# One attention unit per half tile instead of one per tile, in a hybrid mLSTM and windowed-attention layer

## The reference

```
u = rmsnorm(x) * (1 + scale) + shift
aq, ak, av, az, mq, mk, mv, mo, mz, mg, ga, gb = split(u @ w_in)      # 2048 -> 11792 columns
att = windowed attention of 16 query heads / 4 key heads x 64, sink logit, latents also see all context keys
y_b = att * silu(az)
y_a = bidirectional mLSTM(mq, mk, mv, gates mg), 4 heads x 256, head norm, * sigmoid(mo) * silu(mz)
merged = sigmoid(ga) * (y_a @ w_proj_a) + sigmoid(gb) * (y_b @ w_proj_b)
y = x + gate * rmsnorm(merged @ w_out)
```

## Time and profile before

| | us |
|---|---|
| median of 3 runs | 2192.31 |
| the profiled execution's own time | 2192.95 |
| its span | 2191.2 |
| TensorE busy in the span | 2115.9 |
| VectorE, ScalarE busy | 869.0, 643.8 |

### The profile page before, as it was taken

One profiled execution on the slowest core, in us unless ns is written; L12 is line 12 of the kernel. 1 busy time (PEld: TensorE's weight loads), 2 busy tenths in 40 slices (PEclk: granted clock), 3 DMA queues, 4 the chain that ended last, 5 costly groups with the idle time before them and its releaser, 6 DMA issues.

```text
span 2191.2 us, 33985 instructions
## 1 busy us (share of the span) xinstructions
PE 2115.9 (97%) x13450; PEld 1965.6 (90%) x13450; DVE 869.0 (40%) x1674; ACT 643.8 (29%) x1046; POOL 109.4 (5%) x188
## 2 busy tenths in 40 slices
PE   5889999999999999999999979999999999999997
PEld 1559999989999999999999979999999999997885
DVE  5875655432224223322322234343434533352223
ACT  5763122232223332332332221313131422231221
POOL 2001000000000000000000000000000100000001
PEclk9999999999999999999999999999999999999998
DMA  8873765542233224222422243535252644423223
GB/s 299 271 241 112 214 176 169 168 117 82 84 109 92 76 76 127 85 78 76 128 76 76 77 124 78 158 84 158 80 152 85 197 125 124 118 86 125 77 77 144
DMA packets 295171, 274.07 MB, mean 125 GB/s; under 512 B 17921, under 2 KB 243961, under 8 KB 292641
## 3 DMA queue, kind: packets, MB, share of 16 engines
q1 hardware_dynamic: 282416, 218.21, 35.2%
q0 software_dynamic: 12656, 54.40, 6.7%
HBM read 232.65 MB, written 39.92 MB: 124 GB/s over the span
## 4 chain that ended last, share of the span: by engine, by line
PE 92%; DVE 3%; DMA 2%; ACT 1%; issue 1%; SPq 1%; DVEq 0%; POOL 0%; ACTq 0%; POOLq 0%
PE bank L1432 45%; PE bank L1438 22%; PE bank L1651 10%; PE bank L1526 2%; PE bank L1347 2%; PE bank L1402 2%; PE bank L1575 2%; PE bank L1566 1%; PE bank L1577 1%; PE bank L1386 1%; PE bank L1499 1%; DVE WL L893 1%; DMA Y<-in_x_prompt_dram 1%; PE bank L1481 1%; DVE XL L893 1%
## 5 line engine op out<-in xcount | busy, mean ns | idle before, releaser
L1432 PE MATMUL bank<-XH,WH 128*128 128x320 f32 x3392 | 788.1, 314 | 5.5 <-ACT WH L639 4.5
L1432 PE MATMUL bank<-XL,WH 128*128 128x320 f32 x3392 | 773.8, 309 | 0.0
L875 DVE TENSOR_TENSOR WL<-RAW,WH 128x1024 fp32r<-128x1024 f32 x244 | 298.8, 1225 | 988.9 <-ACT WH L639 988.3
L639 ACT ACTIVATE WH<-RAW 128x1024 fp32r<-128x1024 f32 x244 | 258.3, 1059 | 1170.9 <-PE bank L1438 1013.6
L1432 PEld LDWEIGHTS bank<-XH,WH 128*128 128x128 f32 x3392 | 565.6, 188 | 14.1 <-ACT WH L639 5.4
L1432 PEld LDWEIGHTS bank<-XL,WH 128*128 128x128 f32 x3392 | 568.2, 188 | 0.0
L1438 PE MATMUL bank<-XH,WL 128*128 128x320 f32 x3392 | 532.2, 309 | 0.0
L1438 PEld LDWEIGHTS bank<-XH,WL 128*128 128x128 f32 x3392 | 506.2, 188 | 0.0
L1651 PE MATMUL bank<-WH,XH 128*128 128x512 f32 x320 | 127.8, 399 | 3.4 <-DVE WL L875 2.5
L1651 PE MATMUL bank<-WH,XL 128*128 128x512 f32 x320 | 124.7, 390 | 0.0
L1651 PE MATMUL bank<-WL,XH 128*128 128x512 f32 x320 | 124.6, 389 | 0.0
(11 more groups left out here) (196 smaller groups left out, 1510.2 us busy)
## 6 DMA issues: line engine op xcount, KB each, us to landing
RAW<-in_w_in_dram SPq DMA_DIRECT2D x180, 512.0 KB, 4.9
proj_dram<-OUTS POOLq DMA_DIRECT2D x92, 320.0 KB, 3.9
WORK<-in_w_ada_dram SPq DMA_DIRECT2D x54, 512.0 KB, 4.2
RAW<-in_w_ada_dram SPq DMA_DIRECT2D x42, 512.0 KB, 5.2
RAW<-in_w_out_dram SPq DMA_DIRECT2D x32, 512.0 KB, 3.9
WORK<-proj_dram SPq DMA_DIRECT2D x20, 640.0 KB, 4.8
WORK<-proj_dram POOLq DMA_DIRECT2D x32, 320.0 KB, 4.9
RAW<-in_w_proj_a_dram SPq DMA_DIRECT2D x16, 512.0 KB, 4.1
```

The source lines that it names most:

```text
L639: nc.scalar.activation(WH[:, gs % 2, :], RAW[:, slot, :], ACT.Copy).then_inc(hi_done, 1)
L875: V.tensor_tensor(WL[:, gs % 2, :], RAW[:, gs % 4, :], WH[:, gs % 2, :].bitcast(F32), ALU.subtract).then_inc(lo_done, 1)
L1432: pe.matmul(banks[n][:, 0:HALF_TOK], wh[:, k, :], x[:, k0 + k, n * HALF_TOK:(n + 1) * HALF_TOK], start=(first and k == 0 and wi == 0), sto ...
```

## The change

L1 shrinks from 12 to 8 tiles per pass. The 16 tiles that it gives up are run in a plain loop of four times four tiles (`T_LM`) between L0 and L1, with no attention beside them. All 10 units of a head stay in its pass, now one per half: in half s TensorE runs S of unit s-3, the first half of the high products, T of unit s-4, the second half of the high products, A of s-4, the low products, O of s-4. O goes into `ab[3]` and no longer `ab[0]`. VectorE runs `gated` of s-5 first, then `row_max` of s-3, then `lo`, then `normalise` of s-4 and `denominators` of s-3; ScalarE runs `soft` of s-3 and `copy_pt` of s-4 in every half. `RDEN` has two places. SyncE's wait for the gate sums now stands behind the loads of the plain loop.

```
-T_L0, T_L1, T_L2, T_MERGE, T_OUT, T_END = 2, 18, 66, 90, 106, 122
-L1_TILES, L2_TILES = 12, 6
+T_L0, T_LM, T_L1, T_L2, T_MERGE, T_OUT, T_END = 2, 18, 34, 66, 90, 106, 122
+L1_TILES, L2_TILES = 8, 6
...
@@ SyncE
             with sp.Fori(1, 4) as ch:
                 l0_body(ch)
+            with sp.Fori(0, 4) as j:
+                for k in range(4):
+                    in_tile(T_LM + k, 4 * j, 512 * j + (COL_M + P * k))
             sp.wait_ge(gada_used, 32)
...
@@ ScalarE
-                    if s >= 3 and s % 2 == 1 and (s - 3) // 2 < 10:
-                        soft((s - 3) // 2)
-                    if s >= 4 and s % 2 == 0:
-                        copy_pt((s - 4) // 2)
+                    if 0 <= s - 3 < 10:
+                        soft(s - 3)
+                    if 0 <= s - 4 < 10:
+                        copy_pt(s - 4)
...
@@ VectorE
                 for s in range(2 * L1_TILES):
-                    lo(kv, 2 * L1_TILES, 2 * T_L1 + s + 1)
+                    if 0 <= s - 5 < 10:
+                        gated(s - 5)
                     if s == 2:
                         prepare()
                         z_gate()
...
+                    if 0 <= s - 3 < 10:
+                        row_max(s - 3)
+                    lo(kv, 2 * L1_TILES, 2 * T_L1 + s + 1)
+                    if 0 <= s - 4 < 10:
+                        normalise(s - 4)
+                    if 0 <= s - 3 < 10:
+                        denominators(s - 3)
...
@@ TensorE, scores: one wait fewer; probs_transposed: one more; out_transposed: another bank
-                    if u >= 2:
-                        pe.wait_ge(yb_done, 10 * kv + u)
...
+                        pe.wait_ge(yb_done, 10 * kv + u + 1)
...
-                    if u < 9:
-                        pe.wait_ge(neg_max, 10 * kv + (u + 2))
-                    transpose(ab[0][:, 0:P], OB).then_inc(ot_psum, 1)
+                    transpose(ab[3][:, 0:P], OB).then_inc(ot_psum, 1)
...
+                    if 0 <= s - 3 < 10:
+                        scores(s - 3)
+                    if x == 0:
+                        pe.wait_ge(out_ready, L1_TILES * kv + (T_L1 + t - 1))
+                    pe.wait_ge(hi_done, done)
+                    high_products(banks, x, 8 * x, range(0, 4), x == 0)
+                    if 0 <= s - 4 < 10:
+                        probs_transposed(s - 4)
+                    high_products(banks, x, 8 * x, range(4, 8), x == 0)
+                    if 0 <= s - 4 < 10:
+                        attend(s - 4)
+                    pe.wait_ge(lo_done, done)
+                    low_products(banks, x, 8 * x, x == 1).then_inc(w_used, 1)
+                    if 0 <= s - 4 < 10:
+                        out_transposed(s - 4)
```

More of the change, by code:

```diff
@@ L243, in hybrid_layer @@
         RT = work(512)
-        MX = work(8)
-        NM, SE, RSUM, RDEN = MX[:, 0:2], MX[:, 2:4], MX[:, 4:6], MX[:, 6:8]
+        MX = work(10)
+        NM, SE, RSUM, RDEN = MX[:, 0:2], MX[:, 2:4], MX[:, 4:6], [MX[:, 6:8], MX[:, 8:10]]
         MXR = work(2)
@@ L561, in _ @@
                     spill(T_L0 + k, 4 * ch, 4 * ch + (4 + k))
+            with pool.Fori(0, 4) as j:
+                for k in range(4):
+                    spill(T_LM + k, 4 * j, 4 * j + (RB_MQ + k))
             pool.wait_ge(gacc_stored, 16)
@@ L570, in _ @@
                 for k in range(L1_TILES):
-                    row = RB_GA + k + 2 * g if k < 2 else RB_MQ + (k - 2) + 10 * g
+                    row = RB_GA + k + 2 * g if k < 2 else RB_MQ + (16 + k - 2) + 6 * g
                     spill(T_L1 + k, L1_TILES * g, row)
@@ L731, in _ @@
                     hi(ch, 8, 2 * (T_L0 + k) + 1)
-            hi(0, 0, 2 * T_L1)
+            hi(0, 0, 2 * T_LM)
+            with act.Fori(0, 4) as j:
+                for k in range(4):
+                    evac(4 * j, T_LM + k - 1)
+                    hi(j, 8, 2 * (T_LM + k) + 1)
+                    hi(j, 8, 2 * (T_LM + k) + 2)
             with act.Fori(0, KV_HEADS) as kv:
@@ L1025, in _ @@
                 gates.leave(4)
-            lo(0, 0, 2 * T_L1)
+            lo(0, 0, 2 * T_LM)
+            with dve.Fori(0, 4) as j:
+                for k in range(4):
+                    lo(j, 8, 2 * (T_LM + k) + 1)
+                    lo(j, 8, 2 * (T_LM + k) + 2)
             with dve.Fori(0, KV_HEADS) as kv:
@@ L1075, in denominators @@
                     dve.wait_ge(probs, 10 * kv + (u + 1))
-                    chain.link(V.tensor_tensor(RDEN, RSUM, SE, ALU.add))
-                    chain.link(V.reciprocal(RDEN, RDEN))
+                    chain.link(V.tensor_tensor(RDEN[u % 2], RSUM, SE, ALU.add))
+                    chain.link(V.reciprocal(RDEN[u % 2], RDEN[u % 2]))
                 def normalise(u):
@@ L1098, in _ @@
                         z_gate()
-                    if s % 2 == 0 and s >= 6:
-                        gated((s - 6) // 2)
-                    if s % 2 == 1 and s >= 5:
-                        normalise((s - 5) // 2)
-                    if s % 2 == 1 and 3 <= s < 23:
-                        row_max((s - 3) // 2)
-                        denominators((s - 3) // 2)
-                gated(9)
+                    if 0 <= s - 3 < 10:
[5 more added lines that the diff above has]
+                        denominators(s - 3)
                 chain.leave(KV_HEADS)
@@ L1420, in _, with high_products @@
                     start_tiles(g, j, part)
-            def product(banks, wslot, k0, done, first, last, k_wait=None):
+            def high_products(banks, wslot, k0, ks, first):
                 wh = WH[:, wslot, :].rearrange("p (k n) -> p k n", k=8)
-                wl = WL[:, wslot, :].rearrange("p (k n) -> p k n", k=8)
-                pe.wait_ge(hi_done, done)
-                for k in range(8):
-                    if k_wait is not None:
-                        pe.wait_ge(k_wait, k0 + k + 1)
+                for k in ks:
                     for wi, x in enumerate((XH, XL)):
@@ L1434, in product, with low_products @@
                                       start=(first and k == 0 and wi == 0), stop=False)
-                pe.wait_ge(lo_done, done)
+            def low_products(banks, wslot, k0, last):
+                wl = WL[:, wslot, :].rearrange("p (k n) -> p k n", k=8)
                 for k in range(8):
@@ L1441, in product @@
                 return ins
+            def product(banks, wslot, k0, done, first, last, k_wait=None):
+                pe.wait_ge(hi_done, done)
+                for k in range(8):
+                    if k_wait is not None:
+                        pe.wait_ge(k_wait, k0 + k + 1)
+                    high_products(banks, wslot, k0, (k,), first)
+                pe.wait_ge(lo_done, done)
+                return low_products(banks, wslot, k0, last)
             def half(i2, i, t, x, k_wait=None):
@@ L1470, in _ @@
                 l0_chunk(ch)
+            with pe.Fori(0, 4) as j:
+                for k in range(4):
+                    for x in range(2):
+                        half(8 * j, 4 * j, T_LM + k, x)
             pe.wait_ge(cols_done, 1)
```

22 lines of the change are left out of this document (8 added, 14 removed).

## The result

The changed kernel took 2198.86 us (median of 7 runs, 2195.24 to 2200.11); the kernel before took 2190.96 us beside it (7 runs, 2189.12 to 2193.3). The ratio is 1.0032 with an interval of 1.0021 to 1.0044. **The change makes the kernel slower by 0.32%.** The forecast was 2187.8 us with a range of 2181 to 2198, so both the sign and the range were missed. The profiled execution took 2199.19 us, 6.2 us more than the one of before (2192.95).

What follows compares the result with a forecast made beforehand. TensorE, busy 97% of the span, was taken as the bound, so only its idle or slow time could be gained. Terms: -3.8 - 0.7 + 0 + 0 + 0 = -4.5 us, giving 2187.8 us, range 2181 to 2198.

Steps and rivals of the forecast that it cites:

- Term 1: End of L0: next weights no longer queue behind the store that waits for all gate sums; gain 3.8 us.
- Term 2: First attention loads before the first `prepare`: idle 2.65 instead of 3.38 us, gain 0.7 us; later groups gain nothing.
- Term 5: Return of TensorE's attention loop: the instruction-fetch stall stays; taken as 0, bounds 0 to 3.4 us gained.
- Term 3: Attention steps on TensorE: passages between kinds of step cost the same; taken as 0, bounds -6 to +6 us.
- Term 4: Chain of a unit, now in one half: `copy_pt` ends 0.9 us before A is due; no cost.
- The rival that I had chosen for the slower side: In each unit half, A waits for the copied probabilities; 2208 us at an excess of 0.5 us; chance 0.15.
- the repeat of the loop fits: At the attention loop's returns, 2086 instructions stay on the chip and stalls go: 2184.4 us; chance 0.13.
- the gain of term 1 is not kept: First attention loads meet traffic or longer half clock, or units pay another 0.1 us passage: about 2192 us; chance 0.22.

Runs made afterwards that it cites:

- The first experiment: Changed kernel with SyncE holding a pass's attention loads until the weights of its second half are converted, about 1.4 us into the pass: 2188.45 us.
- the body of 1878: Changed kernel with the low products left out in 8 of the 16 L1 halves of a pass, 512 products fewer: 2141.73 us.
- the body of 1622: Changed kernel with the low products left out in all 16 L1 halves of a pass, 1024 products fewer: 2089.96 us.
- the eighth experiment: Changed kernel with TensorE's attention loop written out and late attention loads, plus S of the next unit moved behind A: 2183.33 us.
- the kernel with added traffic: Kernel before, with SyncE copying 4 times 655 KB DRAM to DRAM after the last weights of each attention pass: 2223.53 us.
- the body of 2006 instructions: Changed kernel without the low products of halves 0, 1, 14 and 15 of every attention pass, 256 products fewer: 2167.79 us.

## Why the prediction was wrong

- **Term 1 was right.** The low products of L0 and the plain loop are 7.04 us apart from 405 to 665 us; the 3.8 us are gone. The store on ScalarE's queue shows that they are had without moving a tile.
- **Term 2 was right for the first group** in direction: 2.1 us for the 0.7 forecast, since the slow stretch became shorter too, which lay in its bounds. **The step that failed is its last sentence**: that the loads of the later groups can now begin at s = 14, and "nothing is gained". The start was foreseen to the half; what I asked was only what the loads gain. I didn't ask what else uses the DMA engines at that moment, though two groups of rows on my own list said that instructions are fetched through them there.
- **Term 5 failed with it.** I took 0 "since ... the stall did not depend on the work beside it". Before, there was no work beside it: the loads were issued from 643.92, as the stall ended, and the packet moved alone, so the trace of before could not show a dependence either way. Nothing in it excluded a loss, yet my bounds were 0 to 3.4 us gained. The term measured +10.4 us: 5.9 of idle time and 4.5 of slow clock. The first experiment takes it back with one wait; the written-out loop removes the returns' whole cost. What in the data holds the packet back stays open (the body of 1878).
- The Trainium skill's rule under term 5 (Runtime: NRT & Kernel Launch, Instruction fetch mechanics) is that a taken branch stalls if its target is outside the current window of two pages; the prediction read the whole room of 2048 instructions as that window. The stall agrees with the bodies that were fetched again, but a window of two pages of 256 does not agree with the body of 1622, whose branch back took 0.2 us. The same section calls the fetch "mostly hidden" at a block's boundary; that agrees with the written-out kernels, which fetch their blocks beside the same loads without a gap, so it is the return that exposes the fetch. Its room of 2048 instructions does not agree: 2006 and 1878 instructions were fetched again in each pass, 1622 were not.
- **Term 3** was off by 0.05 us per unit, 2.1 us, inside its bounds of 6. Its argument that the parts sum to 18.06 us, "so there is no hidden stall", shows nothing: the parts were cut out of that same interval, and any stall would be inside one of them. The row said that S costs a passage of 0.15 us after A. It costs 0.24 after O (0.35 less the 0.11 between transposes), and the eighth experiment takes that back. The Trainium skill's draining at a change of tiling mode (TensorEngine Tiling (Array Packing), Key Properties) agrees with a pause staying at the entry to S; that its size depends on the step before is only in the traces.
- **Term 4 was right.** The margin of A over the copied probabilities was forecast at 0.9 us and is 0.92; no unit waits. The rival that I had chosen for the slower side did not happen, and its chance of 0.15 was the whole of that side.
- Of the rivals, "the repeat of the loop fits" is refuted (10 blocks per pass, from 809.6 to 963.4 us), and "the gain of term 1 is not kept" has the right sum of small things, but none of its mechanisms is the one that cost the time. No rival held the mechanism that decided.

Without the failed step the forecast would have been near the truth: the changed kernel with its loads in the next pass took 2188.45 us, for 2187.8 forecast. That it comes so near is in part luck: term 2 was 1.4 us too small a gain and term 3 left out a loss of 2.1 us, and the two nearly cancel.

## What to carry to other kernels

When an edit lets a transfer start earlier, look at what is fetched in the same microseconds, TensorE's instructions at a loop's return above all; "starts earlier, gains nothing" is a loss if it is ahead of something that TensorE waits for. A stall that the trace shows only in a quiet place has no known price in a busy one, so "no worse than now" is no bound for it. The record of a loop's branch shows the stall directly: 0.2 us where the body stayed, 3.3 to 6.0 us where it was fetched. For a long loop on the bounding engine, writing it out (here four passes) removes the question, and a store that blocks a queue of weight loads is worth moving before anything is restructured.

## What the runs showed of the hardware that was not expected

- **Instruction blocks share the DMA engines with data.** From the packet to TensorE's restart it was 2.6 to 3.0 us at every return that was fetched, in the kernel before and after, with late loads, with added traffic and with shorter bodies. What varied was when the packet moved, counted from the start of the branch: 1.0 us where it was alone (six returns), 2.8 to 3.6 us behind the early loads with bodies of 2134 and 2006 instructions, 1.3 to 1.5 us behind the same loads with 1878. The idle time at a return was 0.9 to 1.3, 2.8 to 3.6 and 1.4 to 1.5 us in the three cases. A wait directly in front of the return delays the fetch too, as the kernel with added traffic shows: its branch was taken only when that wait was over.
- **What idle time did to the clock.** After the waits of 0.9 to 1.3 us at returns the granted clock stayed at 2.4 GHz; after those of 2.8 to 3.6 us in the changed kernel it was at 1.2 GHz for 3.41 us, at all three returns, which cost 1.5 us each. A wait of 2.9 us so cost 4.4. Length alone doesn't decide it: with the body of 2006 instructions the stretch came with two of three such returns, and a wait of 2.4 us before the first `prepare` had it in the changed kernel where one of 2.5 us with ScalarE's store had not.
- **A body of 1878 instructions did not stay, one of 1622 did** (as did the L2 loop of 1427). Bodies of 2134 and 2006 cost 10 blocks per pass, 1878 cost 9. Where between 1622 and 1878 the room ends was not tried.
